# A two-block transformer kernel on one core: where block 2's third weight sum is formed, and where its feed-forward units stand in the queues

## What is computed

```python
# block 1, for each layer and each of its two feed-forwards (D_FF = 2816)
def _swiglu(x, w1, w3, w2):
    return (jax.nn.silu(x @ w1) * (x @ w3)) @ w2

# block 2, for each layer i (D_FF_2 = 4096)
u = jax.nn.relu(rms_norm(h, ff_norm[i]) @ w_ff1[i])
h = h + (u * u) @ w_ff2[i]
```

## Time and profile before

| | |
|---|---|
| median of 3 runs | 1930.71 us (1929.75 to 1932.2) |
| the profiled execution | 1929.22 us |
| its span, first to last instruction | 1927.4 us |
| TensorE, matmuls busy | 1881.1 us (98% of the span) |
| TensorE, weight loads busy | 1538.9 us (80%) |
| VectorE busy | 1494.9 us (78%) |
| ScalarE busy | 1050.0 us (54%) |
| mean granted TensorE clock | 0.996 |

### The profile page before, as it was taken

How to read it: one execution, slowest core, us unless ns; L and a number is a source line. 1 busy time by engine, 2 the same in 40 slices (tenths; PEclk the granted TensorE clock), 3 DMA queues, 4 the chain that set the end, 5 groups by cost and what they waited for, 6 DMA issues and landing times.

```text
span 1927.4 us, 22719 instructions
## 1 busy us (share of the span) xinstructions
PE 1881.1 (98%) x8944; PEld 1538.9 (80%) x8944; DVE 1494.9 (78%) x1663; ACT 1050.0 (54%) x1239; POOL 118.9 (6%) x186
## 2 busy tenths in 40 slices
PE   8999999999999999999999999999999999999999
PEld 7788788887888788878888788787778887777787
DVE  6887766778887888777667888778798766779975
ACT  6555444555555555543564655567655555655553
POOL 2001100001000000110000000011000000100000
PEclk9999999999999999999999999999999999999999
DMA  9865554348764766564445766444385545338651
GB/s 337 266 218 168 203 191 173 141 167 284 240 218 152 241 220 222 185 239 174 142 164 185 252 219 220 151 162 157 130 299 177 197 161 178 121 116 309 181 205 57
DMA packets 179177, 376.99 MB, mean 196 GB/s; under 512 B 7568, under 2 KB 51520, under 8 KB 176256
## 3 DMA queue, kind: packets, MB, share of 16 engines
q1 hardware_dynamic: 170512, 334.85, 49.1%
q0 software_dynamic: 8560, 40.69, 8.7%
HBM read 351.39 MB, written 1.05 MB: 183 GB/s over the span
## 4 chain that ended last, share of the span: by engine, by line
PE 80%; DVE 11%; DMA 3%; ACT 3%; DVEq 1%; issue 1%; SPq 0%; ACTq 0%; POOLq 0%
PE acc L926 49%; PE aux L996 15%; PE aux L926 10%; DVE w_low L2710 3%; DVE w_low L2835 2%; PE aux L941 1%; DMA buf_v<-w_ff 1%; DMA w_raw<-ffn_w 1%; DVE buf_v L2840 1%; PE aux L1364 1%; DVEq L2762 1%; DVE xT_low L2716 1%; DMA buf_u<-buf_val 1%; DMA w_low<-buf_q 1%; PE aux L1211 1%
## 5 line engine op out<-in xcount | busy, mean ns | idle before, releaser
L2710 DVE TENSOR_TENSOR w_low<-w_raw,w_high 128x2048 fp32r<-128x2048 f32 (+1 forms) x246 | 554.1, 2265 | 116.4 <-ACT w_high L1959 113.3
L1959 ACT CAST w_high<-w_raw 128x2048 fp32r<-128x2048 f32 (+1 forms) x246 | 462.2, 1895 | 177.4 <-PE acc L926 155.0
L926 PE MATMUL acc<-w_high,yT_high 128*128 128x512 f32 (+1 forms) x836 | 331.6, 397 | 2.5 <-DVE yT_low L2974 2.0
L926 PE MATMUL acc<-w_high,yT_low 128*128 128x512 f32 (+1 forms) x836 | 325.6, 389 | 0.0
L926 PE MATMUL acc<-w_low,yT_high 128*128 128x512 f32 (+1 forms) x836 | 324.9, 389 | 0.0
L926 PE MATMUL acc<-w_high,xT_high 128*128 128x512 f32 (+2 forms) x752 | 297.9, 396 | 6.9 <-DVE xT_low L2716 4.1
L926 PE MATMUL acc<-w_high,xT_low 128*128 128x512 f32 (+2 forms) x752 | 291.3, 387 | 0.0
L926 PE MATMUL acc<-w_low,xT_high 128*128 128x512 f32 (+2 forms) x752 | 290.9, 387 | 0.0
L926 PEld LDWEIGHTS acc<-w_high,yT_high 128*128 128x128 f32 x836 | 157.0, 188 | 38.2 <-issue 6.6
L926 PEld LDWEIGHTS acc<-w_high,yT_low 128*128 128x128 f32 x836 | 156.9, 188 | 33.0
L926 PEld LDWEIGHTS acc<-w_low,yT_high 128*128 128x128 f32 x836 | 157.2, 188 | 30.0
(11 more groups left out here) (411 smaller groups left out, 2754.5 us busy)
## 6 DMA issues: line engine op xcount, KB each, us to landing
w_raw<-w_in SPq DMA_DIRECT2D x52, 1024.0 KB
w_raw<-ffn_w SPq DMA_DIRECT2D x44, 1024.0 KB
w_raw<-w_ff SPq DMA_DIRECT2D x40, 1024.0 KB
w_raw<-ffn_w SPq DMA_DIRECT2D x78, 512.0 KB
buf_u<-buf_val POOLq DMA_DIRECT2D x18, 1024.0 KB, 7.0
w_raw<-w_branch SPq DMA_DIRECT2D x16, 1024.0 KB
buf_q<-ffn_w SPq DMA_DIRECT2D x12, 1024.0 KB, 6.6
buf_v<-ffn_w SPq DMA_DIRECT2D x12, 1024.0 KB, 8.5
```

What stands on the lines that cost most here:

```text
L926: last = nc.tensor.matmul(dst, lhs[:, kt, tok], rhs(j), start=(kt == k_first and q == 0), stop=(kt == k_last and q == 2))
L1959: nc.scalar.copy(whi[:, s, 0:size], raw[:, s, 0:size]).then_inc(slot_hi[s], 1)
L2710: V.tensor_tensor(wlo[:, s, 0:size], raw[:, s, 0:size], cast(whi[:, s, 0:size]), ALU.subtract)\
```

## The change

It has two parts.

**Block 2, both passes of `ffn2`.** The sum Y is no longer formed by VectorE but by a second accumulating DMA on GpSimd's queue, R21 into R11's buffer, behind the wait for X's low part, counted in a new semaphore `y_sum`. VectorE thus does two sums per quad (`sums2_before`), and SyncE's reload of R21 waits on `y_sum`. Along with it the order of units is new: in quad 0, TensorE does `d0_1` between `v_0` and `x_0` instead of before `plain_T(1)`, all of `d1_0` behind `x_0`, and half of `d1_1` behind `w_0`; in quads 1 and 2 the filling moves up by one place. The slots follow the new order, and ScalarE's, VectorE's and SyncE's lists are rewritten to it.

**Block 1, first `ffn1` only, `first`.** ScalarE and VectorE split the transposed first chunk before `b11_0`'s weights instead of after, and quad 0's W is added by VectorE (`w_first`), so the first of the DMAs for W is gone.

```diff
 def ffn2_units():
     order = ["h0_0", "h0_1", "h1_0", "h1_1", "d0_0", "d0_1",
-             "b11_0", "b21_0", "v_0", "x_0", "d1_0", "w_0", "y_0", "b22_0", "d1_1"]
+             "b11_0", "b21_0", "v_0", "w_0", "x_0", "d1_0", "y_0", "b22_0", "d1_1"]
...
# SyncE
                 if q > 0 and r == R21:
-                    sp.wait_ge(sum_done, 3 * quads2_before(i, q - 1) + 3)
+                    sp.wait_ge(y_sum, y_sums_before(i, q))
...
-                for name in ("d1_0", "e0_0", "e0_1", "d1_1"):
+                for name in ("d1_0", "d1_1", "e0_1"):
                     load_ffn2(i, name)
-                for r in (R21, R12, R11, R22):
+                for r in (R21, R12, R11):
                     quad_load2(i, 1, r)
+                load_ffn2(i, "e0_0")
+                quad_load2(i, 1, R22)
...
# GpSimd, block 1, then block 2
-                for q in range(QUADS):
+                for q in range(1 if l == 0 and which == 0 else 0, QUADS):
...
                             pool.dma_start(sum_raw[R12], sum_raw[R22], accum_op=ALU.add).then_inc(w_sum, 16)
+                            s, n_x = ffn2_unit(i, f"x_{q}")
+                            pool.wait_ge(slot_lo[s], n_x + 2)
+                            pool.dma_start(sum_raw[R11], sum_raw[R21], accum_op=ALU.add).then_inc(y_sum, 16)
...
# TensorE, ffn2
                 down("d0_0")
-                down("d0_1")
                 plain_T(1)
...
                     block_product(ffn2_unit(i, f"v_{q}"), 3, *form(f, 0), True)
+                    down("d0_1" if q == 0 else fill[0])
                     pe.wait_ge(quad_act, terms + 1)
                     block_product(ffn2_unit(i, f"x_{q}"), 1, *form(f, 2), False)
-                    if q == 0:
-                        down_part("d1_0", 0)
-                    else:
-                        down(fill[0])
+                    down("d1_0" if q == 0 else fill[1])
                     pe.wait_ge(quad_act, terms + 2)
                     block_product(ffn2_unit(i, f"w_{q}"), 1, *form(f, 1), False)
+                    late = "d1_1" if q == 0 else fill[3]
                     if q == 0:
-                        down_part("d1_0", 1).then_inc(unit_used, 1)
+                        down_part(late, 0)
                     else:
-                        down(fill[1])
+                        down(fill[2])
...
                     block_product(ffn2_unit(i, f"b22_{q}"), 3, *form(f, 3), False)
-                    late = "d1_1" if q == 0 else fill[3]
-                    down_part(late, 0)
                     quad_T(q, 0)
+                    if q > 0:
+                        down_part(late, 0)
                     down_part(late, 1).then_inc(unit_used, 1)
                     quad_T(q, 1)
...
# ScalarE, ffn2, quad 0 of the new list (used, high_plain and high_sum as before)
+                    if q == 0:
+                        used("b21_0")
+                        high_plain("d1_0")
+                        used("d0_1")
...
+                    act.wait_ge(w_sum, 16 * quads2_before(i, q))
                     high_sum("w", q, R12)
...
                     used(f"x_{q}")
                     nc.scalar.copy(term2, aux[:, 1, :]).then_inc(quad_act, 1)
+                    if q == 0:
+                        high_plain("d1_1")
+                    act.wait_ge(y_sum, y_sums_before(i, q) + 16)
                     high_sum("y", q, R11)
...
# VectorE, ffn1 when first
                     low_sum("x", q, R11)
+                    if first and q == 0:
+                        dve.wait_ge(r_full[R22], 16)
+                        V.tensor_tensor(sum_raw[R12], sum_raw[R12], sum_raw[R22], ALU.add).then_inc(w_first, 1)
```

More of the change, by code:

```diff
@@ L124, in ffn2_units @@
     order = ["h0_0", "h0_1", "h1_0", "h1_1", "d0_0", "d0_1",
-             "b11_0", "b21_0", "v_0", "x_0", "d1_0", "w_0", "y_0", "b22_0", "d1_1"]
-    done = ["h0_0", "h1_0", "d0_0", "d0_1",
-            "b11_0", "b21_0", "v_0", "x_0", "w_0", "d1_0", "y_0", "b22_0", "d1_1"]
+             "b11_0", "b21_0", "v_0", "w_0", "x_0", "d1_0", "y_0", "b22_0", "d1_1"]
+    done = ["h0_0", "h1_0", "d0_0",
+            "b11_0", "b21_0", "v_0", "d0_1", "x_0", "d1_0", "w_0", "y_0", "b22_0", "d1_1"]
     for q in range(1, QUADS2):
@@ L2059, in ffn2 @@
                 plain_high_T(1)
-                used("d0_1")
+                used("b11_0")
                 summed(0, 2)
@@ L2183, in ffn1 @@
                     .then_inc(b21_neg, 1)
+                first = l == 0 and which == 0
+                if first:
+                    activate(1, 0)
+                    plain_high_T(0)
                 used("h1_0")
@@ L2186, in ffn1 @@
                 high_sum("b11", 0, R11)
-                activate(1, 0)
-                plain_high_T(0)
+                if not first:
+                    activate(1, 0)
+                    plain_high_T(0)
                 for n in range(FORMS):
@@ L2889, in ffn2 @@
                 multiply(1, 1)
-                low_plain("d0_1")
                 add_to(0, R11, R12)
                 low_sum("b21", 0, R21)
+                form_low(f, 0)
                 low_sum("v", 0, R11)
+                low_plain("d0_1")
                 add_to(0, R11, R22)
-                for n in range(FORMS):
+                for n in range(1, FORMS):
                     form_low(f, n)
+                low_sum("x", 0, R11)
                 plain_low_T(1)
@@ L2920, in ffn2 @@
-                    V.tensor_tensor(silu1, silu1, aux[:, 1, :], ALU.mult).then_inc(h_ready, 1)
                     if q + 1 < QUADS2:
-                        low_sum("b11", q + 1, R11)
-                        add_to(q + 1, R11, R12)
-                        low_sum("b21", q + 1, R21)
+                        if q == 0:
+                            low_sum("b11", 1, R11)
+                        else:
+                            low_sum("b21", q + 1, R21)
+                        dve.wait_ge(quad_act, terms + 4)
@@ new lines, in ffn2 @@
+                        V.tensor_tensor(silu1, silu1, aux[:, 1, :], ALU.mult).then_inc(h_ready, 1)
+                        if q == 0:
+                            add_to(1, R11, R12)
+                        dve.wait_ge(unit_used, ffn2_done(i, f"b22_{q}"))
+                        V.tensor_tensor(term2, aux[:, 3, :], term2, ALU.subtract).then_inc(quad_read, 1)
+                        squared_relu(term2, combined + 3)
+                        if q > 0:
+                            low_sum("b11", q + 1, R11)
+                            add_to(q + 1, R11, R12)
@@ L2925, in ffn2 @@
+                        quad_low_T(q, 0)
+                        if q == 0:
+                            low_sum("b21", 1, R21)
+                        low_sum("v", q + 1, R11)
+                        quad_low_T(q, 1)
+                        add_to(q + 1, R11, R22)
                     else:
                         tail = [f"e{q}_{k}" for k in range(4)]
+                        dve.wait_ge(quad_act, terms + 4)
+                        V.tensor_tensor(silu1, silu1, aux[:, 1, :], ALU.mult).then_inc(h_ready, 1)
@@ L3006, in ffn1 @@
                 low_plain("d0")
+                first = l == 0 and which == 0
+                if first:
+                    dve.wait_ge(aux_full[2], n_aux[2].k + 1)
+                    plain_low_T(0)
                 low_sum("b11", 0, R11)
-                dve.wait_ge(aux_full[2], n_aux[2].k + 1)
-                plain_low_T(0)
+                if not first:
+                    dve.wait_ge(aux_full[2], n_aux[2].k + 1)
+                    plain_low_T(0)
                 multiply(1, 0)
```

108 lines of the change are left out of this document (59 added, 49 removed).

## The result

The changed kernel takes 1955.43 us (median; 1954.22 to 1956.66) against 1930.23 us of the kernel before on the same chip: 1.0129 times, 95% interval 1.0112 to 1.0147. It is slower, as forecast, but by twice the forecast's amount, and outside its range. The profiled execution has a span of 1953.5 us, 26.1 more than before. The sum had 11.9.

A forecast was written before the change was run, and what follows sets the result against it. It took TensorE's gaps to bound the kernel, VectorE setting the end in quad 0. Terms of +5.5 us (first `ffn2`), +9.6 (second) and -3.2 (block 1) summed to +11.9, forecasting 1942.5 us, range 1936 to 1948.

The forecast's parts named there:

- `v_0`: Quad 0 of both `ffn2`: TensorE stands 9.2 us at `v_0` for `plain_low_T(1)`, late in VectorE's list.
- The clock: Behind the 9.2 us wait at `v_0`: half clock costs 2.0 us, bounds 0 and 3.2.
- 4.4 us after TensorE resumed: Old kernel, first `ffn2`: half clock after the 3.2 us wait ended 4.4 us after TensorE resumed.
- Seam of quad 0: Quad 0 to quad 1 in `ffn2`: waits of 1.0 us before the first transposes and 2.1 us for `e0_0`.
- Block 1: First `ffn1`: waits of 1.1, 1.7 and 1.7 us replace longer ones; `w_0` ends 3.2 us sooner.
- Y by DMA ... In quads 1 and 2 that buys nothing ... 1 us left: Block 2: sparing VectorE 2.2 us per quad buys nothing in quads 1 and 2; a 10.9 us transfer leaves 1 us.
- TensorE does not wait there: Quads 1 and 2 of `ffn2`: TensorE has no wait, so VectorE's spared 2.2 us per quad buys nothing.
- the seam from quad 1 to 2: Block 2: `e1_0`'s low part is ready at 14.6 us, TensorE there at 15.4, no wait.
- Rival 3: Y's DMA takes over 16.7 us beside quad 1's loads, each us beyond costs one per pass; 1949 at 20 us; chance 0.05.
- Rival 1 (the relief decides): Quad 0: `v_0` is not held by bank 3 and starts at 1410.15; median 1927.0 us, faster; chance 0.08.
- The sign I gave for a late transfer: The forecast is wrong if a wait ended by the DMA into `buf_v` stands among the longest.
- No wait on `y_sum`: New trace: no wait on `y_sum` appears; in quad 0 Y's DMA is hidden with 5.8 us to spare.

The follow-up runs named there:

- A undone: Changed kernel with `plain_low_T(1)` right behind v_0's low part again on VectorE, ahead of `d0_1`'s: 1943.84 us, 1.0062 times the kernel before.
- block 1 alone: The kernel before with only the change's part in the first `ffn1`: 1929.24 us, 0.9988 times the kernel before.
- The first run: Changed kernel with only `plain_low_T(1)` moved back right behind v_0's low part on VectorE: 1943.84 us, 1.0062 times the kernel before.
- the Relu first: Changed kernel with `plain_low_T(1)` behind v_0's low part, `e0_3`'s load ahead of the reloads, quad 0's Relu and product ahead of `b11_1`: 1927.90 us, 0.9987.

## Why the forecast was wrong

- **`v_0`: right.** Forecast 9.2 us and 0.55 more in the second pass; measured 8.98 and 9.58, which with the 0.16 us that a bracket leaves out are 9.14 and 9.74. Taking VectorE's new list row by row with old durations gave it to 0.1 us.
- **The clock: right.** 2.0 us each forecast, 2.3 measured; the 1.3 behind the second quad 1 were not forecast. The Trainium skill ("TensorE: Matmul & The Clock Gate", Part 1) says that the throttled clock is the default and that activity releases it; the two long waits agree with it, and with A undone the clock at `v_0` stayed at 1.00. After short waits no rule of that kind showed: of thirteen of 2.3 us nine were followed by half clock (block 1 alone, above). The prediction's "4.4 us after TensorE resumed" counts from `b11_1`; from the end of the 3.2 us wait (1445.62) to 1452.87 it is 7.2.
- **Seam of quad 0: right in sum.** 1.0 and 2.1 forecast, 1.12 and 1.35 measured, with small ones between. The first `ffn2` up to `e0_0` cost 6.1 (forecast 5.5), the second 10.2 (9.6).
- **Block 1: nearly right.** Three waits of 1.1, 1.7, 1.7 forecast, 1.26, 1.43, 1.52 measured; 3.2 us forecast, 2.8 measured behind `w_0` and 2.95 at the start of block 2. Alone it brought less, some 2 us. (The old trace moves 337 GB/s in its first 48 us against 196 on the mean, so weights do not arrive slowly there in sum; W's transfer took 12.0 us.)
- **"Y by DMA ... In quads 1 and 2 that buys nothing ... 1 us left": this step failed.** The transfer was even faster than assumed, 8.0 and 9.1 us in the two quads 1 instead of 10.9, and `y_1`'s operand was in time. What was priced was Y's way to its own reader. What stood behind the new wait on its queue wasn't: R21's reload, R12's, and `e0_3`'s load (9.60 us), whose cast the change had put ahead of `term3`'s copy. That is 5.4 and 7.0 us, 12.4 in all. "TensorE does not wait there" was read from the old order's rows, and the new order of the casts and loads in quads 1 and 2 got no term at all; it makes a little over half of this cost (Y back on VectorE, above). The same step counted the seam from quad 1 to 2 as no wait; it is 0.43. Its reading that the slowest such sum took 10.9 us is wrong too: in the old trace W took 12.0 us in the first `ffn1` (1 MB as well) and 11.3 in the second `ffn2`.
- **The rivals.** Rival 3 (Y's transfer late) had the right place, but for the wrong reason, the transfer's length; its price of 1 us for each us beyond 16.7 was not what happened. The 16.7 is the room of quad 0 alone (1418.1 to 1434.8); by the prediction's own count quads 1 and 2 leave 11.9. Rival 1 (the relief decides) asked for the kernel in which `v_0` isn't held. The first run made it: 1943.8, not 1927, because of quad 1 and the seam of 4.78 us. The sign I gave for a late transfer, a wait of TensorE ended by the DMA into `buf_v`, did not come although the transfer had its part: TensorE's waits name ScalarE's copy and VectorE's low part, and the transfer stands four steps further back, in the chain. "No wait on `y_sum`" did not hold either: ScalarE idled 1.42 us for it ahead of `y_1`'s cast, and SyncE's reload of R21 went out as Y landed.

## What to carry to other kernels

When a wait on a slow transfer is added to a queue, list all that is queued behind it and price each item by its own reader, not only the reader of the transfer. A move in one engine's list has to be checked together with the other lists: here neither SyncE's order nor ScalarE's cost much alone. After a long wait is removed, expect the next one to show, and ask what sets it before counting the full gain; here half came back.

## What the runs showed of the hardware

Ahead of one instruction near 637 us TensorE waits 2.29 to 2.31 us in all thirteen profiled executions; half clock of 3.41 us followed in nine and not in four, so a gain of 2 us elsewhere can be lost to it 600 us later (12 matmuls instead of 19 in 3.41 us). After the eight waits of 9 us (four kernels, two passes) it lasted 10.24 us seven times, of which 5.1 us fell on work in the changed kernel, and 13.65 us once, with 6.2 on work (`e0_3`'s load ahead, second pass).

The accumulating transfer of 1 MB took 7.0 to 9.1 us for Y in the changed kernel and up to 9.9 with the Relu first; for W it took 6.9 to 12.0 in the kernel before, 7.0 in the median. The 1 MB reload of R21 behind Y took 5.3 us with no other load under way; seven loads into these buffers that were issued within 5 us behind two others took 6.9 to 10.0 (10.0 in the earlier trace rows), and the load of `e0_3` 9.6.
